# Attention output products issued one by one behind their transposes, with four turned tiles in place of seven

## What is computed

```
def nsa(q, k_cmp, v_cmp, k_slc, v_slc, k_win, v_win, gates, ...):
    s = einsum('bgrqd,bgnd->bgrqn', qi, ck) * scale
    p_c = masked_softmax(s, cmp_end[None, :] <= t[:, None])
    o_c = einsum('bgrqn,bgnd->bgrqd', p_c, cv)
    ...
    p_s = masked_softmax(s, smask[:, :, None])
    o_s = einsum('bgrqk,bgqkd->bgrqd', p_s, vsel)
    ...
    p_w = masked_softmax(s, wmask)
    o_w = einsum('bgrqk,bgkd->bgrqd', p_w, vwi)
    ...
    o = gates[..., 0:1] * o_c + gates[..., 1:2] * o_s + gates[..., 2:3] * o_w
```

## Time and profile before

| | |
|---|---|
| median of three runs | 1639.93 us (1639.77 to 1643.47) |
| time of the profiled execution | 1639.93 us |
| its span, first to last instruction | 1638.1 us |
| mean granted TensorE clock | 0.991 |
| TensorE busy | 1593.7 us, 97% |
| VectorE busy | 939.6 us, 57% |
| ScalarE busy | 592.1 us, 36% |

### The profile page before, as it was taken

One profiled execution on the slowest core, in us unless ns is written; L12 is line 12 of the kernel. 1 busy time (PEld: TensorE's weight loads), 2 busy tenths in 40 slices (PEclk: granted clock), 3 DMA queues, 4 the chain that ended last, 5 costly groups with the idle time before them and its releaser, 6 DMA issues.

```text
span 1638.1 us, 22283 instructions
## 1 busy us (share of the span) xinstructions
PE 1593.7 (97%) x8486; PEld 1313.2 (80%) x8486; DVE 939.6 (57%) x1615; ACT 592.1 (36%) x1030; POOL 77.9 (5%) x126
## 2 busy tenths in 40 slices
PE   8999999999889999999999999999999999999997
PEld 6888888889766777688888888888888888888885
DVE  7834556563777776543456565656565656566342
ACT  6114343345666776722322122212221222133221
POOL 0111221121000000000000000000000000000000
PEclk9999999999799999999999999999999999999999
DMA  6423233236000000330221112111211121122001
GB/s 224 136 97 122 84 117 100 83 97 213 27 17 14 14 14 2 132 113 0 78 77 40 38 38 77 38 38 38 77 38 38 40 76 38 38 78 103 26 39 39
DMA packets 53242, 110.61 MB, mean 68 GB/s; under 512 B 13104, under 2 KB 22320, under 8 KB 53168
## 3 DMA queue, kind: packets, MB, share of 16 engines
q1 hardware_dynamic: 45744, 85.47, 15.8%
q0 software_dynamic: 7424, 24.12, 4.4%
HBM read 89.65 MB, written 19.92 MB: 67 GB/s over the span
## 4 chain that ended last, share of the span: by engine, by line
PE 93%; DVE 3%; issue 2%; ACT 1%; DMA 0%; DVEq 0%; POOLq 0%; POOL 0%; SPq 0%; ACTq 0%
PE ps L1574 28%; PE ps L1190 15%; PE ps L1192 15%; PE ps L1191 15%; PE ps L1305 5%; PE ps L1479 4%; PE ps L1434 2%; PE ps L1440 2%; PE ps L1561 1%; PE ps L1195 1%; PE ps L1358 1%; PE ps L1442 1%; DVE nb L1964 0%; PE ps L1259 0%; PE ps L1274 0%
## 5 line engine op out<-in xcount | busy, mean ns | idle before, releaser
L2138 DVE TENSOR_TENSOR h<-h,ps 128x512 f32<-128x512 f32 x336 | 224.3, 686 | 137.9 <-PE ps L1192 136.2
L1574 PE MATMUL ps<-hth,wul 128*128 128x512 f32 x672 | 206.9, 389 | 0.0
L1574 PE MATMUL ps<-htl,wuh 128*128 128x512 f32 x672 | 206.9, 389 | 0.0
L1574 PE MATMUL ps<-hth,wuh 128*128 128x512 f32 x672 | 206.9, 389 | 0.0
L1190 PE MATMUL ps<-wh,xth 128*128 128x512 f32 (+1 forms) x448 | 185.0, 413 | 7.6 <-DVE wl L1708 7.6
L1192 PE MATMUL ps<-wh,xtl 128*128 128x512 f32 (+1 forms) x448 | 170.1, 380 | 0.0
L1191 PE MATMUL ps<-wl,xth 128*128 128x512 f32 (+1 forms) x448 | 169.2, 378 | 0.0
L1134 ACT ACTIVATE ffh<-ffa 128x1024 fp32r<-128x1024 f32 x22 | 23.3, 1061 | 358.3 <-DVE ffa L2165 358.3
L1574 PEld LDWEIGHTS ps<-hth,wul 128*128 128x128 f32 x672 | 126.1, 188 | 26.2
L1574 PEld LDWEIGHTS ps<-hth,wuh 128*128 128x128 f32 x672 | 126.1, 188 | 26.2
L1574 PEld LDWEIGHTS ps<-htl,wuh 128*128 128x128 f32 x672 | 126.1, 188 | 26.2
(11 more groups left out here) (261 smaller groups left out, 2932.4 us busy)
## 6 DMA issues: line engine op xcount, KB each, us to landing
wuraw<-in_w_up SPq DMA_DIRECT2D x44, 512.0 KB, 5.2
wraw<-in_w_in SPq DMA_DIRECT2D x48, 256.0 KB, 3.3
proj_d<-stage POOLq DMA_DIRECT2D x48, 256.0 KB, 2.3
wdraw<-in_w_down SPq DMA_DIRECT2D x22, 512.0 KB, 3.5
rin<-proj_d POOLq DMA_DIRECT2D x32, 256.0 KB, 4.5
xraw<-in_xt SPq DMA_DIRECT2D x16, 256.0 KB, 6.3
owraw<-in_w_out SPq DMA_DIRECT2D x8, 512.0 KB, 5.8
h<-in_x SPq DMA_DIRECT2D x1, 4096.0 KB, 16.4
```

The lines of the kernel that those rows point to most:

```text
L1574: mm = nc.tensor.matmul(ps[:, 2 * part + half, :], w_, x_[:, k, half * 512:(half + 1) * 512], start=(k == 0 and i == 0), stop=(k == NK - 1 ...
L2138: nc.vector.tensor_tensor(hh, hh, ps[:, 4 + o_ % 4, :], ALU.add).then_inc(dn_add, 1)
```

## The change

The ring of turned tiles gets four places in place of seven. The order of a unit's steps is a plain list: a tile is turned, and from the third on each turn is followed by the output step of the tile two before; the last two output steps stand at the end. The steps are spread over the unit's eight slots by their number. PVS and PV_LAG go.

```diff
-        NPT = 7
+        NPT = 4
         ptf = a.put("ptf", [P, NPT, 2, 2 * P], F32)
...
-        PVS, PV_LAG = 4, 2
...
             for v in range(NV):
                 base = per * (v + 1) + 1
+                tail = []
+                if v % 2 == 0:
+                    tail.append(("turn_ret", v // 2))
                 n = len(key_tiles(v))
-                tail = [[("turn_ret", v // 2)]] if v % 2 == 0 else []
-                done = 0
-                for j in range(n):
-                    tail.append([("turn_p", v, j)])
-                    if j + 1 >= done + PVS + PV_LAG:
-                        tail.append([("output", v, k) for k in range(done, done + PVS)])
-                        done += PVS
-                if done < n:
-                    tail.append([("output", v, k) for k in range(done, n)])
-                total, at = sum(len(unit) for unit in tail), 0
-                for unit in tail:
-                    slots[base + per * at // total].extend(unit)
-                    at += len(unit)
+                for j in range(n + 2):
+                    if j < n:
+                        tail.append(("turn_p", v, j))
+                    if j >= 2:
+                        tail.append(("output", v, j - 2))
+                for x, st in enumerate(tail):
+                    slots[base + per * x // len(tail)].append(st)
                 slots[base + per - 1].append(("close", v))
```

## The result

| | median us | low to high |
|---|---|---|
| before, beside it | 1640.0 | 1639.77 to 1643.47 |
| changed | 1650.22 | 1650.11 to 1651.16 |

The ratio is 1.0059, 95% interval 1.0043 to 1.0076, so 7 to 12 us slower. The forecast was 1660.0 us with a range of 1649 to 1670: the direction was right, the time lies at the low edge of the range, and the step of + 20.1 us was twice too long.

A forecast was written before the change was run, and what follows sets the result against it. TensorE was taken to bound the kernel: 94 more runs at 0.31 us add 29.1 us, 9.0 us of waits for exponentials come back, so + 20.1 on 1639.9 gives 1660.0 us, range 1649 to 1670.

The forecast's parts named there:

- What bounds the kernel: Whole kernel: TensorE, busy 97% of the span and 93% of the chain; its added work is paid unless it waits.
- 94 more runs, 0.31 us each: Unbroken runs of output steps on TensorE go from 36 to 130; entering and leaving them adds 29.1 us.
- Rival A: Output steps on TensorE: a single run pays only the entry, + 3.2 us, 1643 us; chance 0.09.
- C: Single output steps wait for their ScalarE copy, early slack gives nothing back: + 35.7 us, 1676 us; chance 0.10.
- NPT at no cost: Ring of turned tiles, NPT from 7 to 4: ScalarE copies' new wait is hidden, costed at nothing.
- The cover: TensorE's waits for exponentials before score products, up to 540 us: all 9.0 us come back.
- Waits for retl: TensorE's waits for retl in the stage: not given back, they stay at 5.9 us in all.
- Half clock in two stretches: Half-clock stretch between 431.9 and 438.8 us: such a stretch may come or go for one to three microseconds.
- The shape in time: Stage up to v = 8 longer by 1 to 4 us, v = 9 to 15 by 2 to 3 us each.
- Rival D: All 12.0 us of TensorE's idle time up to 540 us come back: + 16.2, 1656 us; chance 0.13.

The follow-up runs named there:

- the ring of seven: The changed kernel (spread order) with its ring of turned tiles put back from four places to seven: 1650.74 us.
- the full-width pair: Output steps as one matmul with 128 weight columns, in the order of before (grouped) and of the change (spread): 1702.84 and 1681.90 us.
- the split kernel: Order of before, with a small 128*128 matmul between neighbouring output steps of units 8 to 15: 1659.29 us, ratio 1.0122.
- boundaries tried here (2, 8 and 9): Kernel before with the change's order in units below 2, 8 or 9 and old groups from there on: 1636.75, 1634.72 and 1636.59 us.
- Each order in its own half: Kernel before with the change's order in units 0 to 7 and old groups in 8 to 15: 1634.72 us, ratio 0.9961.

## Why the prediction was wrong: the price held, the cover did not

**What bounds the kernel: right.** TensorE is the chain before and after, and every microsecond of the stage reaches the end.

**94 more runs, 0.31 us each: right.** The single run costs 0.30 to 0.35 us in the changed profile, a split 0.29. The parts below take the lower figure, 94 x 0.29 = 27.3 us; with the 29.1 of the sum all that was given back would be 1.8 us more. Rival A, the cheap single run, is excluded; so is C: TensorE's matmuls wait nowhere for ptf, and its weight loads wait 4.8 us for it in the stage (1.6 at the output steps, 3.2 at score products), 4.5 before.

**NPT at no cost: right**, by the ring of seven.

**The cover: the step that failed.** "I let all 9.0 us come back", and the kernel got back 27.3 - 10.3 = 17.0 us. This is the term that was mis-sized: subtracted at 9.0 us, measured at 17.0 (18.8 at the higher run price). About 13 of them lie before unit 8: 26 more runs there should have cost 7.5 us, and the stretch became 5.6 us shorter at equal work. The parts that the runs show:
- Waits for exponentials, 9.0 to 1.9 us: 7.1 us, the term as I had it.
- Waits for retl, which I had left at 5.9: 4.7 now, 1.2 us. Waits for normalized probabilities went the other way, from 1.2 to 2.3.
- Half clock in two stretches, 2.7 to 2.9 us between the profiles. I had it as a possible one to three microseconds to either side, outside the sum.
- The rest, some 7 us, stands in no idle row.

Part of this rest is hidden in the way the rows count: a wait runs there from the modelled end of the matmul before it, and that end is late. At 534.29 the row says 1.17 us idle. The matmul before it, in the timeline of the kernel before:

```profile
532.88 0.23 PE L1442 MATMUL ps<-masks_b,ident_b 128*128 128x128 bf16 x1
```

It started 1.41 us earlier, and the same pair undisturbed takes 0.04 (0.03 in the rounded), so 1.37 us were lost. Measured in this way, from start to start and less what the same pair takes undisturbed, TensorE's waits from unit 1's second slot on sum to 25.9 us before and 13.4 after: 12.5 us. This is an estimate. It depends on which time of a pair is called undisturbed, and other choices give a difference of 6 to 12 us. Part of it is the clock's again, because a pair at half clock counts as a disturbed one. So at least 2 to 4 us of the 17.0 stay unexplained, and with the lower choices up to half of them.

That the spacing gives time back, and is not only something found beside it, is shown by the full-width pair (20.9 us for spreading when a run is free) and by the split kernel, which pays for 74 runs, spreads nothing, and loses 19.6 of 20.3 us. That it is waits of TensorE is shown for the 7.1 us in the rows, and the clock's part for the two stretches; for the rest it is argued.

**The shape in time: half right.** I had the first part 1 to 4 us longer; it is 5.8 us shorter. Units behind it (the prediction's query tiles v are the units) were to take 2 to 3 us more each; the rest of the stage, with the steps of the nine units 7 to 15, took 16.1 more in all, 1.8 for each. Rival D, more early slack, was the nearest, and even it let back only 12.0 us, TensorE's whole idle time by the same rows. That the measured time still fell inside the range is owed to the room left toward rival A, whose reason, a cheap single run, was not the one that filled it.

## What to carry over

An order has two prices, and they are found separately: count the changes of array form (weight columns or rows per matmul) and price each from a run in the trace; then measure waits from start to start, not by the idle column. Where the engine has slack, single steps spread evenly are worth their changes of form; where it has none, keep steps of one form together. Of the boundaries tried here (2, 8 and 9), 8 is the best; those between 2 and 8 were not tried. Each order in its own half beats both kernels, before by 0.4%. And when two medians differ by a few microseconds, compare the granted clock of the executions first.

## What was not expected of the hardware

- Two plain float32 matmuls with 64 weight columns and 256 columns each, side by side on the two halves of the partitions, take 0.43 us together; the same work as one matmul with 128 weight columns and 512 columns takes 0.86 us. The half-width form is twice as fast for this work, and its price is the 0.30 us at entering and leaving.
- Going from 128 to 63 rows inside a run of output steps costs 0.14 us, and padding to 128 rows takes the cost away. With full width, going to 63 rows and back costs 0.46 us.
- Half-clock stretches of 3 to 7 us appear in one execution and not in another with the same order up to there; two of them cost 2.7 to 2.9 us. In 61 executions of the kernel before, the time went from 1638.2 us at a mean clock of 0.992 to 1645.6 us at 0.988.
